# An encoder layer on one core: the first projection in pieces of two token tiles, and another order of three engines before the first recurrent gates

## The chip, the cores and the metric

The kernel runs on 1 core of a Trainium2 chip. The metric is the device time of one execution in microseconds (us), here the median of several. The engines work in parallel, each through its own instruction queue in order, and wait for one another on semaphores: TensorE (PE, its weight loads are PEld), VectorE (DVE), ScalarE (ACT), GpSimd (POOL), and SyncE (SP), which issues the transfers.

## The reference, cut to what matters

One layer over 2304 tokens (2048 of one sequence, 256 of another) with 1024 features, and a final norm:

```python
h = rmsnorm(x, norm1_g)
z = h @ w_in                       # 14 column tiles of 128
u_pool, u_lru, u_gate, u_conv = z[..., :o1], z[..., o1:o2], z[..., o2:o3], z[..., o3:]
y_pool = pool_mixer(u_pool, pool_w, pool_scale)
c = depthwise_conv(u_lru, lru_conv_w, lru_conv_b, 2, 1)          # 4 taps
y_lru = (rg_lru(c, ..., False) + rg_lru(c, ..., True)) * gelu(u_gate)
a, g = split(u_conv)                                             # conformer_conv
v = depthwise_conv(a * sigmoid(g), dw_w, dw_b, 15, 15)           # 31 taps
v = silu(group_norm(v, gn_g, gn_b, 4))
y_conv = v @ pw_w + pw_b                                         # 256 -> 256
x = x + concat([y_pool, y_lru, y_conv]) @ w_out
x = x + expert_choice_ffn(rmsnorm(x, norm2_g), ...)              # 16 experts
return rmsnorm(x, final_g)
```

## The kernel before

Channels lie on the 128 partitions and the tokens along the free dimension. `rows[:, r, :]` is one row tile: 128 channels by all 2304 tokens, with padding (2320 elements between `LO` and `HI`). TensorE's work on a row is cut in the five segments of `SEG`: four of 512 tokens and one of 256. Segment `s` uses PSUM bank `s`; ScalarE moves it to `rows` (an evacuation). `seg_full` counts filled segments, `seg_out` evacuated ones, and a matmul group into a bank waits for the evacuation of what was there.

The order of work is written out by hand, engine by engine. The stages that the change touches:

1. **Norm and first projection.** 18 token tiles of 128 are loaded. For each, ScalarE squares it in four parts (`n1_squares`, L763), TensorE sums these with one small matmul (`n1_stat_of`, L1053), ScalarE takes the root (`n1_root`, L768), and VectorE takes the reciprocal, scales the tile and transposes it into `normT` (L1351, L1363; `n1_tr` counts). Meanwhile TensorE projects two column tiles, g = 0 (`a0`) and g = 1 (the gate `g0`), from `w_ring[:, g]` (`first_piece`, L1066). Each segment and g has 8 matmuls in two halves of four, and one statistic matmul is issued behind every half. Segment `s` waits for tiles up to 4s + 3. ScalarE evacuates (`first_evac`, L774). The last sequence part of g has the sigmoid applied straight from PSUM, the rest in one pass over the row (L789). Behind them ScalarE takes Abs and Exp of the `lambda` vectors (L799, L800), from which VectorE works out a softplus on 128 x 8 (L1381 to L1395).
2. **31-tap convolution.** VectorE multiplies `a` by the sigmoid (L1414), then runs 31 taps over the full row (L1417, L1420), for channel tile 0 and then for tile 1. Between taps 9 and 10, and 20 and 21, of tile 1 it subtracts the group means of tile 0 (`centre`, L1407). Meanwhile TensorE projects the tiles `G_A1`, `G_G1`, `G_P0`, `G_P1`, `G_U`, `G_GT` (`z_tile`, L1098) and works out group means (`mean_of`, L1115) and variances (`var_of`, L1122).
3. **From the last tap to the first gates.** For channel tile i: `gn_mult` (VectorE, L1456), `gn_affine` (ScalarE, two row passes, L831 and L833), `gn_silu` (VectorE, L1461; `gn_out` counts). Between them lie the pool mixer (`pool_mix`, VectorE, L1470 to L1486; `G_PM0`, `G_PM1` on TensorE), the pointwise projection (`G_PW0`, `G_PW1`, `pw_sb`: each of the two outputs sums over both channel tiles), and the preparation of the first recurrent tile: `lru_conv` (four taps over `G_U`'s row, L1437, L1439), and the high and low parts of `u` and of the gate weights (`u_high`, L846; `bd_high`, L841; and L1447, L1450 on VectorE). ScalarE waits for the stores of rows 2 and 4 (`mix_st[2]`, `mix_st[3]`) before the loop.
4. **Loop over four recurrent tiles** (`lru_tile`): four gates (TensorE L1085, ScalarE L899) and two further column tiles (TensorE L1098). The output projection, the router, the experts (16, the largest part) and the final norm follow.

`evac` in the tables of the profile is L806, `gn_square` L817, `gn_scale`'s last pass L824.

Of the kernel before, what the change touches and what calls it, by code (L numbers as in the profile page):

```python
# [22 lines left out]
F32 = mybir.dt.float32  # L23
# [60 lines left out]
N_X, N_SQ, N_LEAD = 6, 3, 6  # L84
# [51 lines left out]
def encoder_layer(nc, x, consts, vecs, norm1_g, w_in, pool_w, lru_wa, lru_wx, conv_pw_w, w_out,  # L136
                  norm2_g, router_w, w_gate, w_up, w_down, final_g, y):
    ctx = ExitStack()
    with ctx:
# [188 lines left out]
        n1_xld = [sem_of(f"n1_xld{q}") for q in range(N_X)]  # L328
        n1_squared, n1_stat = sem_of("n1_squared"), sem_of("n1_stat")
# [56 lines left out]
        first_bank = lambda g, s: 2 * g + s % 2  # L386

# [42 lines left out]
        def _(sp_eng):  # L430
# [75 lines left out]
            store_row(4, 7, 3)  # L506
# [170 lines left out]
        def _(pool):  # L677
# [12 lines left out]
            e.wait_ge(seg_full, NS * (G_PW1 + 1))  # L690
# [59 lines left out]
        def _(act):  # L750
# [20 lines left out]
            def first_evac(g, s, func=ACT.Identity):  # L771
                t0, c0, n = SEG[s]
                e.wait_ge(seg_full, 2 * s + g + 1)
                e.activation(rows[:, g, c0:c0 + n], ps[:, first_bank(g, s), 0:n], func).then_inc(seg_out, 1)  # L774
# [6 lines left out]
            for t in range(2, NT):  # L781
# [3 lines left out]
                if t >= 7 and t % 2 == 1:  # L785
                    first_evac((t - 7) // 2 % 2, (t - 7) // 4)
            done = SEG[NS - 2][1]
            e.wait_ge(seg_out, 2 * NS - 4)
            e.activation(rows[:, 1, PAD:done], rows[:, 1, PAD:done], ACT.Sigmoid).then_inc(glu_sig, 1)  # L789
            for s in range(NS - 2, NS):  # L790
                first_evac(0, s)
                first_evac(1, s, ACT.Sigmoid)

# [6 lines left out]
            e.activation(sp[:, 1, :, :], sp[:, 0, :, :], ACT.Exp, scale=-1.0).then_inc(sp_ready, 1)  # L800

# [55 lines left out]
            evac(G_GT, 8, ACT.Identity, between=((0, lambda: gn_affine(0)), (3, lambda: gn_square(1))))  # L857
            gn_scale(1)
            evac(G_PM0, 10, ACT.Identity, scale=vec[:, V_PSC:V_PSC + 1])
            gn_affine(1)  # L860
            evac(G_PM1, 11, ACT.Identity, scale=vec[:, V_PSC + 1:V_PSC + 2])
# [26 lines left out]
            def lru_tile(l, last):  # L888
# [151 lines left out]
        def _(pe):  # L1040
# [15 lines left out]
            def first_piece(s, g, half):  # L1056

                t0, c0, n = SEG[s]
                if half == 0 and s >= 2:
                    e.wait_ge(seg_out, 2 * (s - 2) + g + 1)  # L1060
                if half == 0 and g == 0:
                    e.wait_ge(n1_tr, min(4 * s + 4, NT))
                if half == 0 and s == 0:
# [855 lines left out]
```

## Time and profile before

| what | value |
|---|---|
| median of 3 runs | 2691.8 us (2690.86 to 2691.93) |
| the profiled execution's own time | 2687.19 us |
| its span, first to last instruction | 2685.3 us |
| busy: PE / DVE / ACT / POOL | 2484.8 / 1749.7 / 1137.1 / 493.3 us |
| mean granted TensorE clock | 0.966 of full speed |

The profiled execution is 4.6 us shorter than the median of the runs. Instants in the rows further down are from the start of its span. The stages above take the first 357.5 us up to the first `z_tile` of the loop; all that follows is the same program in both kernels but for one wait and one call that is split in two.

### The profile page before, as it was taken

Reading aid. Unit: us, or ns where it says so; the run is one execution under the profiler, and the core shown is the slowest. Engines: PE = TensorE matmul, PEld = TensorE weight load, DVE = VectorE, ACT = ScalarE, POOL = GpSimd, SP = SyncE. Lnnn points to the kernel's source line nnn.
Section 4 is the critical chain, followed back from the end, with each engine's and each line's share of the span. In section 5 each row is a group of like instructions: output and inputs, shape, how many; then the busy total and the mean of one; then the engine's idle time right before and its main releaser. Section 6 shows DMA issues by size and latency. Waiting matters only on the chain.

```text
span 2685.3 us, 42869 instructions
## 1 busy us (share of the span) xinstructions
PE 2484.8 (93%) x15834; PEld 2185.8 (81%) x15834; DVE 1749.7 (65%) x2114; ACT 1137.1 (42%) x1645; POOL 493.3 (18%) x347
## 2 busy tenths in 40 slices
PE   6999899989996299999999999999999999999990
PEld 3544455558786299999999999999999999999980
DVE  6699766678456676666656765756666667557544
ACT  5102555552232144454444444444544444444433
POOL 0000033310000112132132131321321321312201
PEclk9999999999997599999999999999999999999995
DMA  8000111137765176686776866866867767768638
GB/s 174 24 16 9 53 36 35 35 127 219 263 229 169 57 200 165 191 210 158 205 196 158 219 175 166 226 166 190 216 161 196 205 160 208 188 162 223 168 82 296
DMA packets 656264, 425.30 MB, mean 158 GB/s; under 512 B 30592, under 2 KB 633216, under 8 KB 655104
## 3 DMA queue, kind: packets, MB, share of 16 engines
q1 hardware_dynamic: 628480, 385.46, 49.7%
q0 software_dynamic: 27648, 37.77, 7.4%
q8 instruction: 117, 1.92, 0.3%
q14 instruction: 19, 0.16, 0.0%
HBM read 357.09 MB, written 66.06 MB: 158 GB/s over the span
## 4 chain that ended last, share of the span: by engine, by line
PE 83%; DVE 11%; issue 2%; ACT 2%; DMA 2%; SPq 1%; POOL 0%; ACTq 0%; DVEq 0%; POOLq 0%
PE ps L1302 42%; PE ps L1319 21%; PE ps L1098 7%; DVE rows L1420 6%; PE ps L1174 4%; PE ps L1189 4%; PE ps L1066 2%; PE ps L1206 1%; DMA fin_x<-resid 1%; PE ps L1085 1%; DVE over_t L1676 1%; ACT rows L899 1%; PE ps L1047 1%; DVE wo_l L1505 0%; SPq L450 0%
## 5 line engine op out<-in xcount | busy, mean ns | idle before, releaser
L1302 PE MATMUL ps<-x_h,w_l 128*128 128x288 f32 x2816 | 831.2, 295 | 18.6 <-issue 18.6
L1302 PE MATMUL ps<-x_l,w_h 128*128 128x288 f32 x2816 | 829.9, 295 | 0.0
L1302 PE MATMUL ps<-x_h,w_h 128*128 128x288 f32 x2816 | 829.7, 295 | 0.0
L1707 DVE TENSOR_TENSOR w_l<-raw,w_h 128x1024 fp32r<-128x1024 f32 (+1 forms) x480 | 637.4, 1328 | 277.3 <-ACT w_h L982 276.7
L982 ACT ACTIVATE w_h<-raw 128x1024 fp32r<-128x1024 f32 (+1 forms) x480 | 545.4, 1143 | 453.1 <-PE ps L1319 272.4
L1302 PEld LDWEIGHTS ps<-x_h,w_l 128*128 128x128 f32 x2816 | 530.0, 188 | 18.7 <-issue 18.7
L1302 PEld LDWEIGHTS ps<-x_l,w_h 128*128 128x128 f32 x2816 | 530.2, 188 | 0.0
L1302 PEld LDWEIGHTS ps<-x_h,w_h 128*128 128x128 f32 x2816 | 530.1, 188 | 0.0
L734 POOL DMA_INDIRECT resid<-y_rows,idx_cur x144 | 250.2, 1738 | 964.9 <-ACT y_rows L997 930.4
L1319 PE MATMUL ps<-h_l,w_h 128*128 128x288 f32 x1408 | 414.4, 294 | 0.0
L1319 PE MATMUL ps<-h_h,w_h 128*128 128x288 f32 x1408 | 414.4, 294 | 0.0
L1319 PE MATMUL ps<-h_h,w_l 128*128 128x288 f32 x1408 | 414.4, 294 | 0.0
L1098 PE MATMUL ps<-normT,w_ring 128*128 128x512 f32 (+1 forms) x960 | 372.9, 550 | 2.1 <-issue 1.1
L1098 PEld LDWEIGHTS ps<-normT,w_ring 128*128 128x128 f32 x960 | 182.5, 190 | 190.7 <-issue 184.4
L1319 PEld LDWEIGHTS ps<-h_h,w_h 128*128 128x128 f32 x1408 | 264.6, 188 | 0.0
L1319 PEld LDWEIGHTS ps<-h_h,w_l 128*128 128x128 f32 x1408 | 264.6, 188 | 0.0
L1319 PEld LDWEIGHTS ps<-h_l,w_h 128*128 128x128 f32 x1408 | 264.5, 188 | 0.0
L719 POOL DMA_INDIRECT gathered<-tokens,idx_next x144 | 153.7, 1067 | 580.6 <-issue 379.3
L1009 ACT ACTIVATE sig<-ps 128x288 f32<-128x288 f32 x176 | 72.1, 410 | 291.1 <-PE ps L1302 291.0
L1789 DVE TENSOR_TENSOR h_l<-hid,h_h 128x288 fp32r<-128x288 f32 x176 | 80.5, 457 | 149.2 <-ACT h_h L1014 147.6
L1814 DVE STREAM_TRANSPOSE y_rows<-ps 128x288 f32<-128x288 f32 x128 | 61.7, 482 | 161.3 <-PE ps L1319 160.2
L1420 DVE SCALAR_TENSOR_TENSOR rows<-rows,vec 128x2320 f32<-128x2320 f32 x60 | 158.1, 2635 | 2.1
(230 smaller groups left out, 2484.7 us busy)
## 6 DMA issues: line engine op xcount, KB each, us to landing
raw<-w_gate SPq DMA_DIRECT2D x176, 512.0 KB, 4.2
raw<-w_up SPq DMA_DIRECT2D x176, 512.0 KB, 4.7
raw<-w_down SPq DMA_DIRECT2D x128, 704.0 KB, 5.9
n_x<-x SPq DMA_DIRECT2D x72, 128.0 KB, 5.0
e_x<-x SPq DMA_DIRECT2D x18, 512.0 KB, 4.6
resid<-e_x SPq DMA_DIRECT2D x18, 512.0 KB, 3.0
s_x<-resid SPq DMA_DIRECT2D x18, 512.0 KB, 4.5
resid<-s_r SPq DMA_DIRECT2D x18, 512.0 KB, 3.0
```

Of the source, the lines that this page charges most:

```text
L719: e.indirect_dma_start(gathered[:, c, :], None, token_parts, bass.IndirectOffsetOnAxis(ap=idx_next[:, c:c + 1], axis=0)).then_inc(x_got[c ...
L734: e.indirect_dma_start(resid_parts, bass.IndirectOffsetOnAxis(ap=idx_cur[:, c:c + 1], axis=0), y_rows[:, c, :], None, compute_op=ALU.add). ...
L982: e.activation(w_h[:, m % SPLIT, 0:k * P], raw[:, m % RAW, 0:k * P], ACT.Copy).then_inc(hi_done, 1)
L1009: e.activation(sig[:, j % 2, :], ps[:, 2 * (j % 2), 0:SLOTS], ACT.Sigmoid).then_inc(sig_done, 1)
L1098: ins = e.matmul(ps[:, s, 0:n], w_ring[:, slot, k, :], normT[:, k, t0:t0 + n], start=k == 0, stop=k == KD - 1)
L1174: ins = e.matmul(ps[:, early_bank(t, h), :], lhs[t % E_MIX][:, m, :], rhs[:, k, cols], start=n == 1, stop=n == 12)
L1189: ins = e.matmul(ps[:, 1 + 2 * p + h, :], lhs[:, p, k, :], rhs[:, 2 + k, cols], start=n == 1, stop=n == 3 * LK)
L1302: ins = e.matmul(ps[:, bank, 0:SLOTS], lhs(k), rhs[:, k, 0:SLOTS], start=m == 1, stop=m == 3 * KD)
L1319: ins = e.matmul(ps[:, bank, 0:SLOTS], lhs(k), rhs[:, k, 0:SLOTS], start=m == 1, stop=m == 3 * KF)
L1420: ins = e.scalar_tensor_tensor(out=rows[:, c, mid], in0=rows[:, v, LO - 15 + k:HI - 15 + k], scalar=tap(k), in1=rows[:, c, mid], op0=ALU.m ...
L1707: e.tensor_tensor(w_l[:, m % SPLIT, 0:k * P], raw[:, m % RAW, 0:k * P], w_h[:, m % SPLIT, 0:k * P].bitcast(F32), ALU.subtract).then_inc(lo ...
L1789: e.tensor_tensor(h_l[:, j, 0:SLOTS], hid[:, j % 2, :], h_h[:, j, 0:SLOTS].bitcast(F32), ALU.subtract).then_inc(hl_done, 1)
```

## The change

The first projection is cut in 18 pieces of 256 tokens (`PAIR`), g = 0 and g = 1 by turns, each of 8 matmuls of 128x256, each waiting for two token tiles; it has semaphores of its own (`first_full`, `first_out`). ScalarE takes Abs and Exp, and the sigmoid pass over `g0`, before its last four evacuations. Between the last tap and the gates VectorE, ScalarE and TensorE run in another order, the pointwise projection is split in the part of channel tile 0 and that of tile 1, its second output goes to row 5 instead of 4, and the wait for the stores moves into the loop, ahead of the first write to these rows.

```diff
-N_X, N_SQ, N_LEAD = 6, 3, 6
+N_X, N_SQ, PAIR = 6, 3, 2 * P
+N_SEG = T // PAIR
...
+        first_cols = lambda s: (PAIR * s, PAD + PAIR * s if PAIR * s < SAMPLE else SEQ[1][0])
+        pw_bank = lambda j, s: (NS * j + s) % 8
...
             def w_load(n, c):
-                if n == 2:
-                    e.wait_ge(seg_full, 2 * NS - 1)
-                elif n > 2:
+                if n in (2, 3):
+                    e.wait_ge(first_full, 2 * N_SEG - 3 + n)
+                elif n > 3:
...
-            store_row(4, 7, 3)
+            store_row(5, 7, 3)
...
             e.wait_ge(gn_out, 2)
-            e.wait_ge(seg_full, NS * (G_PW1 + 1))
             e.memset(rows[:, 0:6, PAD + SAMPLE:PAD + SAMPLE + PAD], 0.0).then_inc(rows_zeroed, 1)
...
             def first_evac(g, s, func=ACT.Identity):
-                t0, c0, n = SEG[s]
-                e.wait_ge(seg_full, 2 * s + g + 1)
-                e.activation(rows[:, g, c0:c0 + n], ps[:, first_bank(g, s), 0:n], func).then_inc(seg_out, 1)
+                t0, c0 = first_cols(s)
+                e.wait_ge(first_full, 2 * s + g + 1)
+                e.activation(rows[:, g, c0:c0 + PAIR], ps[:, first_bank(g, s), 0:PAIR], func).then_inc(first_out, 1)
...
-                if t >= 7 and t % 2 == 1:
-                    first_evac((t - 7) // 2 % 2, (t - 7) // 4)
-            done = SEG[NS - 2][1]
-            e.wait_ge(seg_out, 2 * NS - 4)
-            e.activation(rows[:, 1, PAD:done], rows[:, 1, PAD:done], ACT.Sigmoid).then_inc(glu_sig, 1)
-            for s in range(NS - 2, NS):
-                first_evac(0, s)
-                first_evac(1, s, ACT.Sigmoid)
-
+                if t >= N_X + 1:
+                    first_evac((t - N_X - 1) % 2, (t - N_X - 1) // 2)
+            for n in range(NT - N_X - 1, 2 * N_SEG - 4):
+                first_evac(n % 2, n // 2)
             e.wait_ge(cst_ld, 16)
             e.wait_ge(vec_ld, 16)
...
             step.link(e.activation(sp[:, 0, :, :], lam, ACT.Abs))
             e.activation(sp[:, 1, :, :], sp[:, 0, :, :], ACT.Exp, scale=-1.0).then_inc(sp_ready, 1)
+            done = first_cols(N_SEG - 2)[1]
+            e.wait_ge(first_out, 2 * N_SEG - 4)
+            e.activation(rows[:, 1, PAD:done], rows[:, 1, PAD:done], ACT.Sigmoid).then_inc(glu_sig, 1)
+            for s in range(N_SEG - 2, N_SEG):
+                first_evac(0, s)
+                first_evac(1, s, ACT.Sigmoid)
+            e.sem_inc(seg_out, 2 * NS)
...
-            evac(G_GT, 8, ACT.Identity, between=((0, lambda: gn_affine(0)), (3, lambda: gn_square(1))))
+            evac(G_GT, 8, ACT.Identity, between=((0, lambda: (gn_affine(0), gn_square(1))),))
             gn_scale(1)
             evac(G_PM0, 10, ACT.Identity, scale=vec[:, V_PSC:V_PSC + 1])
+            evac(G_PM1, 11, ACT.Identity, scale=vec[:, V_PSC + 1:V_PSC + 2])
             gn_affine(1)
-            evac(G_PM1, 11, ACT.Identity, scale=vec[:, V_PSC + 1:V_PSC + 2])
             bd_high(0)
             for s in (0, 1):
                 e.wait_ge(mix_st[s], 32)
-            for i in range(2):
-                e.wait_ge(gn_out, i + 1)
-                evac(G_PW0 + i, C[i], ACT.Identity, bias=vec[:, V_PWB + i:V_PWB + i + 1],
-                     between=((1, lambda: u_high(0)),) if i == 1 else ())
-            for s in (2, 3):
-                e.wait_ge(mix_st[s], 32)
+            u_high(0)
+            e.wait_ge(gn_out, 2)
+            for j in range(2):
+                for s, (t0, c0, n) in enumerate(SEG):
+                    e.wait_ge(seg_full, NS * (G_PW0 + j) + s + 1)
+                    e.activation(rows[:, (2, 5)[j], c0:c0 + n], ps[:, pw_bank(j, s), 0:n], ACT.Identity,
+                                 bias=vec[:, V_PWB + j:V_PWB + j + 1]).then_inc(seg_out, 1)
...
                     r, ex = rows[:, 3 * d, LO:HI], rows[:, 3 * d + 2, LO:HI]
+                    e.wait_ge(mix_st[2 + d], 32)
                     step.link(e.activation(ex, r, ACT.Exp, scale=spc(6, d)))
...
-            for n in range(4 * NS):
-                first_piece(n // 4, n // 2 % 2, n % 2)
-                if N_LEAD + n < NT:
-                    n1_stat_of(N_LEAD + n)
+            for n in range(2 * N_SEG):
+                first_piece(n // 2, n % 2)
+                if N_X + n < NT:
+                    n1_stat_of(N_X + n)
+            e.sem_inc(seg_full, 2 * NS)
...
-            z_first(G_GT, 7, between=((0, lambda: mean_of(1, 0, 1, 2)), (1, lambda: mean_of(1, 3, 4))))
+            z_first(G_GT, 7, between=((0, lambda: mean_of(1, 0, 1, 2, 3, 4)),))
...
+            places = [(j, s) for j in range(2) for s in range(NS)]
+            e.wait_ge(gn_out, 1)
+            for n, (j, s) in enumerate(places[:8]):
+                if n < NS:
+                    e.wait_ge(seg_out, NS * G_PM1 + s + 1)
+                pw_mat(0, j, s)
             e.wait_ge(gn_out, 2)
-            for j in range(2):
-                segments(G_PW0 + j, lambda s, t0, c0, n: [
-                    (pw_sb[:, i, j * P:(j + 1) * P], rows[:, (0, 3)[i], c0:c0 + n]) for i in range(2)])
+            for j, s in places[:8]:
+                pw_mat(1, j, s).then_inc(seg_full, 1)
+            for n, (j, s) in enumerate(places[8:]):
+                e.wait_ge(seg_out, NS * G_PW0 + n + 1)
+                pw_mat(0, j, s)
+                pw_mat(1, j, s).then_inc(seg_full, 1)
+            e.wait_ge(seg_out, NS * (G_PW1 + 1))
...
+            centre(1, 0, 1, 2)
             gn_mult(0)
-            centre(1, 0, 1, 2, 3, 4)
+            centre(1, 3, 4)
+            pool_mix(0)
             gn_silu(0)
-            pool_mix(0)
             pool_mix(1)
             gn_mult(1)
-            gn_silu(1)
             e.wait_ge(seg_out, NS * (G_U + 1))
             lru_conv(0)
+            gn_silu(1)
+            u_low(0)
```

`first_piece(s, g)` is now eight matmuls of 256 tokens that wait for `n1_tr` >= 2s + 2 and, from s = 2 on, for `first_out` >= 2(s - 2) + g + 1. `pw_mat(i, j, s)` is one matmul of input tile i, output j, segment s. `u_low` is the last operation of the old `lru_conv`, now called apart.

Three places of the programs, as the engines have them in their queues. ScalarE at the end of the first projection, before:

```order
L768 ACTIVATE n_dev<-ps 128x4 x2
L774 ACTIVATE rows<-ps 128x512
L789 ACT_TABLE_LOAD
L789 ACTIVATE rows<-rows 128x1536
L774 ACTIVATE rows<-ps 128x512 x2
L774 ACTIVATE rows<-ps 128x256 x2
L799 ACTIVATE sp<-vec 128x8
L800 ACT_TABLE_LOAD
L800 ACTIVATE sp<-sp 128x8
L806 ACTIVATE rows<-ps 128x512 x4
```

and now (`sp` is the softplus scratch, L777 the evacuation of a piece, L811 that of `G_A1`):

```order
L771 ACTIVATE n_dev<-ps 128x4
L777 ACTIVATE rows<-ps 128x256 x4
L797 ACTIVATE sp<-vec 128x8
L798 ACT_TABLE_LOAD
L798 ACTIVATE sp<-sp 128x8
L801 ACT_TABLE_LOAD
L801 ACTIVATE rows<-rows 128x1792
L777 ACTIVATE rows<-ps 128x256 x4
L811 ACTIVATE rows<-ps 128x512 x4
```

Abs and Exp have moved ahead of the last four evacuations, and the row pass of the sigmoid stands behind them.

VectorE from the last operation of the pool mixer to the loop, before (`gn_mult(1)` L1456, `gn_silu(1)` L1461, the four taps, then the two low parts):

```order
L1486 SCALAR_TENSOR_TENSOR rows<-rows,cst 128x2320
L1456 TENSOR_TENSOR rows<-rows 128x2320
L1461 TENSOR_TENSOR rows<-rows 128x2320
L1437 TENSOR_SCALAR rows<-rows,vec 128x2320
L1439 SCALAR_TENSOR_TENSOR rows<-rows,vec 128x2320 x3
L1447 TENSOR_TENSOR bd_parts<-bd_w,bd_parts 128x512
L1450 TENSOR_TENSOR u_parts<-rows,u_parts 128x2320
```

and now (`gn_mult(1)` L1482, taps L1461 and L1463, `gn_silu(1)` L1487, `u_low` L1476):

```order
L1512 SCALAR_TENSOR_TENSOR rows<-rows,cst 128x2320
L1482 TENSOR_TENSOR rows<-rows 128x2320
L1461 TENSOR_SCALAR rows<-rows,vec 128x2320
L1463 SCALAR_TENSOR_TENSOR rows<-rows,vec 128x2320 x3
L1471 TENSOR_TENSOR bd_parts<-bd_w,bd_parts 128x512
L1487 TENSOR_TENSOR rows<-rows 128x2320
L1476 TENSOR_TENSOR u_parts<-rows,u_parts 128x2320
```

The second silu product has moved behind the four taps and the low part of the weights.

TensorE from the pool projections to the loop, before:

```order
L1085 MATMUL ps<-rows,bd_pool 128x512 x4
L1085 MATMUL ps<-rows,bd_pool 128x256
L1085 MATMUL ps<-rows,pw_sb 128x512 x8
L1085 MATMUL ps<-rows,pw_sb 128x256 x2
L1085 MATMUL ps<-rows,pw_sb 128x512 x8
L1085 MATMUL ps<-rows,pw_sb 128x256 x2
```

and now (the first two rows of `pw_sb` and seven of the next are the parts of tile 0 and the start of those of tile 1, which wait for `gn_out` 2):

```order
L1092 MATMUL ps<-rows,bd_pool 128x512 x4
L1092 MATMUL ps<-rows,bd_pool 128x256
L1147 MATMUL ps<-rows,pw_sb 128x512 x4
L1147 MATMUL ps<-rows,pw_sb 128x256
L1147 MATMUL ps<-rows,pw_sb 128x512 x7
L1147 MATMUL ps<-rows,pw_sb 128x256
L1147 MATMUL ps<-rows,pw_sb 128x512 x5
L1147 MATMUL ps<-rows,pw_sb 128x256 x2
```

The number of pointwise matmuls is the same, 16 of 512 and 4 of 256; eight of them (7 of 512, 1 of 256) now stand ahead of the wait for the second silu product.

## Rows read from the trace of the kernel before

**Rows 1.** The page: the chain that ended last, shares by engine.

```profile
PE 83%; DVE 11%; issue 2%; ACT 2%; DMA 2%; SPq 1%; POOL 0%; ACTq 0%; DVEq 0%; POOLq 0%
```

**Rows 2.** Instructions in order, 22 to 34 us: start, duration, engine, [idle before].

```profile
25.47 5.53 PE L1066 MATMUL ps<-normT,w_ring 128*128 128x512 f32 x8 [1.16 <-DVE normT L1351]
...
29.91 0.19 ACT L763 ACTIVATION_READ_ACCUMULATOR n_sq<-n_x 128x1 f32 x1
...
30.84 0.28 PE L1053 MATMUL ps<-n_ss,same_tok 128*128 128x4 f32 x2
```

**Rows 3.** Instructions in order, 60 to 110 us, ScalarE and VectorE.

```profile
85.22 0.60 ACT L774 ACTIVATE rows<-ps 128x512 f32<-128x512 f32 x1 [6.27 <-PE ps L1066]
...
92.12 0.38 ACT L774 ACTIVATE rows<-ps 128x256 f32<-128x256 f32 x1 [3.07 <-PE ps L1066]
...
97.38 2.57 DVE L1414 TENSOR_TENSOR rows<-rows 128x2320 f32<-128x2320 f32 x1
```

**Rows 4.** Instructions in order, 200 to 280 us, TensorE.

```profile
210.63 1.53 PE L1115 MATMUL ps<-rows,cst 128*128 128x512 f32 x4 [1.25 <-DVE rows L1407]
...
257.10 7.03 PE L1098 MATMUL ps<-normT,w_ring 128*128 128x512 f32 x16
268.63 4.27 PE L1115 MATMUL ps<-rows,cst 128*128 128x512 f32 x6 [4.50 <-DVE rows L1420]
```

**Rows 5.** Instructions in order, 280 to 330 us, VectorE.

```profile
280.66 1.02 DVE L1407 TENSOR_TENSOR rows<-rows,ps 128x512 f32<-128x512 f32 x2 [7.04 <-PE ps L1115]
...
284.08 2.60 DVE L1470 TENSOR_TENSOR rows<-rows 128x2351 f32<-128x2351 f32 x1
...
293.85 2.61 DVE L1470 TENSOR_TENSOR rows<-rows 128x2351 f32<-128x2351 f32 x1
...
308.89 2.58 DVE L1456 TENSOR_TENSOR rows<-rows 128x2320 f32<-128x2320 f32 x1
316.21 2.57 DVE L1461 TENSOR_TENSOR rows<-rows 128x2320 f32<-128x2320 f32 x1 [4.74 <-ACT rows L833]
318.70 1.48 DVE L1437 TENSOR_SCALAR rows<-rows,vec 128x2320 f32<-128x2320 f32 x1
...
328.12 0.69 DVE L1447 TENSOR_TENSOR bd_parts<-bd_w,bd_parts 128x512 fp32r<-128x512 f32 x1
```

**Rows 6.** Instructions in order, 300 to 430 us, ScalarE.

```profile
305.94 2.77 ACT L806 ACTIVATE rows<-ps,vec 128x512 f32<-128x512 f32 x5
...
311.51 2.32 ACT L831 ACTIVATE rows<-rows,vec 128x2320 f32<-128x2320 f32 x1 [1.50 <-DVE rows L1456]
...
341.73 1.28 ACT L891 ACT_TABLE_LOAD   x1 [4.96 <-DMA mixed<-rows]
...
344.74 3.36 ACT L899 ACTIVATE rows<-ps,vec_l 128x512 f32<-128x512 f32 x6
...
423.10 8.14 ACT L899 ACTIVATE rows<-ps,vec_l 128x512 f32<-128x512 f32 x15
```

**Rows 7.** Instructions in order, 290 to 435 us, TensorE.

```profile
298.08 4.03 PE L1122 MATMUL ps<-rows,cst 128*128 128x512 f32 x10
...
318.84 17.43 PE L1085 MATMUL ps<-rows,pw_sb 128*128 128x512 f32 x40 [4.09 <-ACT rows L806]
...
345.48 11.76 PE L1085 MATMUL ps<-u_parts,bd_parts 128*128 128x512 f32 x45 [4.49 <-ACT rows L899]
357.50 62.11 PE L1098 MATMUL ps<-normT,w_ring 128*128 128x512 f32 x160 [0.26 <-ACT rows L899]
...
433.90 62.11 PE L1098 MATMUL ps<-normT,w_ring 128*128 128x512 f32 x160 [0.38 <-ACT rows L899]
```

**Rows 8.** Stretches of 1 us: length, PE busy (instructions), granted clock, DMA.

```profile
320.00:321.00 1.00, 1.00 (x2) 0.50 1.10 451
...
348.00:349.00 1.00, 1.00 (x3) 0.50 0.00 0
```

**Rows 9.** The page's costliest groups: weight loads of the column tiles.

```profile
L1098 PEld LDWEIGHTS ps<-normT,w_ring 128*128 128x128 f32 x960 | 182.5, 190 | 190.7 <-issue 184.4
```

More of the change, by code:

```diff
@@ L328, in encoder_layer @@
         n1_xld = [sem_of(f"n1_xld{q}") for q in range(N_X)]
+        first_full, first_out = sem_of("first_full"), sem_of("first_out")
         n1_squared, n1_stat = sem_of("n1_squared"), sem_of("n1_stat")
@@ L1054, in n1_stat_of, with first_piece @@
                          start=True, stop=True).then_inc(n1_stat, 1)
[L1056 to L1063, printed above, removed]
+            def first_piece(s, g):
+                t0, c0 = first_cols(s)
+                if g == 0:
+                    e.wait_ge(n1_tr, 2 * s + 2)
+                if s >= 2:
+                    e.wait_ge(first_out, 2 * (s - 2) + g + 1)
+                if s == 0:
                     e.wait_ge(w_ld[g], 16 * PARTS)
-                for k in range(4 * half, 4 * half + 4):
-                    ins = e.matmul(ps[:, first_bank(g, s), 0:n], w_ring[:, g, k, :], normT[:, k, t0:t0 + n],
+                for k in range(KD):
+                    ins = e.matmul(ps[:, first_bank(g, s), 0:PAIR], w_ring[:, g, k, :], normT[:, k, t0:t0 + PAIR],
                                    start=k == 0, stop=k == KD - 1)
-                if half == 1:
-                    ins.then_inc(seg_full, 1)
+                ins.then_inc(first_full, 1)
             e.wait_ge(same_set, 1)
-            for t in range(N_LEAD):
+            for t in range(N_X):
                 n1_stat_of(t)
-            for n in range(4 * NS):
-                first_piece(n // 4, n // 2 % 2, n % 2)
-                if N_LEAD + n < NT:
-                    n1_stat_of(N_LEAD + n)
+            for n in range(2 * N_SEG):
[3 more added lines that the diff above has]
+            e.sem_inc(seg_full, 2 * NS)
             def segments(g, mats):
@@ L1093, in z_tile @@
                     if isinstance(g, int) and g == G_A1:
-                        e.wait_ge(seg_out, 2 * NS - (s == 0))
+                        e.wait_ge(first_out, 2 * N_SEG - (s < 2))
                     else:
@@ L1137, in _, with pw_mat @@
                 segments(G_PM0 + i, lambda s, t0, c0, n: [(bd_pool[:, i, :], rows[:, 10 + i, c0:c0 + n])])
-            e.wait_ge(gn_out, 2)
-            for j in range(2):
-                segments(G_PW0 + j, lambda s, t0, c0, n: [
-                    (pw_sb[:, i, j * P:(j + 1) * P], rows[:, (0, 3)[i], c0:c0 + n]) for i in range(2)])
+            def pw_mat(i, j, s):
+                t0, c0, n = SEG[s]
+                return e.matmul(ps[:, pw_bank(j, s), 0:n], pw_sb[:, i, j * P:(j + 1) * P],
+                                rows[:, (0, 3)[i], c0:c0 + n], start=i == 0, stop=i == 1)
+            places = [(j, s) for j in range(2) for s in range(NS)]
[4 more added lines that the diff above has]
+                pw_mat(0, j, s)
+            e.wait_ge(gn_out, 2)
+            for j, s in places[:8]:
[5 more added lines that the diff above has]
+            e.wait_ge(seg_out, NS * (G_PW1 + 1))
             def lru_tile(l, last):
@@ L1409, in _ @@
             for i in range(2):
-                e.wait_ge(seg_out, NS * (2 * i + 2))
                 if i == 0:
                     e.wait_ge(glu_sig, 1)
+                    e.wait_ge(first_out, 2 * N_SEG)
+                else:
+                    e.wait_ge(seg_out, NS * (G_G1 + 1))
                 v, c = V[i], C[i]
@@ L1448, in lru_conv, with u_low @@
                                 ).then_inc(bd_lo, 1)
+            def u_low(l):
                 e.wait_ge(u_hi, l + 1)
-                e.tensor_tensor(u_parts[:, 1, mid], c, u_parts[:, 0, mid].bitcast(F32), ALU.subtract
+                e.tensor_tensor(u_parts[:, 1, mid], rows[:, 9, mid], u_parts[:, 0, mid].bitcast(F32), ALU.subtract
                                 ).then_inc(u_lo, 1)
@@ L1587, in lru_tile @@
                     lru_conv(l + 1)
+                    u_low(l + 1)
                     e.wait_ge(mix_st[4], 32 * (l + 1))
```

## The prediction, made before the changed kernel was run

> **What bounds the kernel.** I read the chain of work first: it lies 83% on TensorE and 11% on VectorE [rows 1], and VectorE's part is the 31-tap convolution. Then the instructions in order, engine by engine, to see who waits for whom at the joints of the first 357.5 us. There the bound changes hands: TensorE up to the end of the first projection; VectorE from the start of the convolution at 97.38 [rows 3] to its last tap at 268.6, where TensorE has waited 4.50 us [rows 4]; then a mixed chain of VectorE, ScalarE and TensorE to the first `z_tile` of the loop at 357.50 [rows 7]. From there TensorE runs through, and the two programs are the same. So I ask only how much earlier that `z_tile` starts. No transfer or engine behind it has a clock of its own, so the rest shifts with it.
>
> **Start of the first projection.** Before, the first piece starts at 25.47, after 1.16 us of waiting for the fourth tile [rows 2]. Now it needs two tiles, but stands behind the statistic of tile 5 on TensorE's queue, so it can start at 24.3. The piece is as long as before (eight half-wide matmuls for four wide ones), 5.4 us from its start to the next statistic matmul, 25.47 to 30.84: 29.7. That statistic, of tile 6, needs squares that end at 30.10 (29.91 + 0.19) [rows 2]; these wait for the tile's transfer, which is not moved. So it starts at about 30.15: 0.7 us earlier than before, not 1.2. Later tiles are never late: piece n needs tile n + 1, whose statistic stands behind piece n - 5.
>
> Wide: 8 matmuls of 512 tokens take 6.87 us (6.27 + 0.60, ScalarE's interval between evacuations); 8 of 256 take 3.45 (3.07 + 0.38) [rows 3]. A piece costs 3.45 where half a segment cost 3.435, so 16 pieces add 0.3 us. The stage ends 0.4 us earlier.
>
> On this the Trainium skill speaks against the change. "TensorE: Matmul & The Clock Gate", section "Back-to-back issue gap", adds a fixed 2.5 ns to every pass at full clock. Twice as many matmuls are 64 more; if each makes four passes that is an estimate of 0.6 us, where the rows make it 0.3. The forecast would be 0.3 us longer.
>
> **Start of the convolution.** Before, ScalarE's last evacuation ends at 92.50 and VectorE starts the product only at 97.38 [rows 3]: 4.9 us for Abs, a table load, Exp and the softplus chain. Now Abs and Exp come after the evacuation of piece 13, when four pieces (13.8 us) are still to run. ScalarE's two table loads and the row pass take about 5 us of this and delay one evacuation, which nothing waits for: a piece waits for the evacuation four pieces back. VectorE is idle then. It starts at 92.50 - 0.4 + 0.05 = 92.15, which is 5.2 earlier. If that cover were gone, the 4.9 would be back.
>
> The convolution's own work is the same, so the last tap ends at 268.6 - 5.2 = 263.4. Does TensorE arrive in time? It starts `G_A1` 0.4 earlier (its weights still wait for the last g = 0 piece), and the wait of 1.25 us for `centre` at 210.63 [rows 4] goes, since VectorE is now 5.2 ahead there. Its first `G_GT` segment ended at 264.13 (257.10 + 7.03) [rows 4]; now at 262.5. It waits 0.9 us instead of 4.5, and I expect no fall of its clock there. A shift beyond 6.1 would gain nothing more without TensorE.
>
> **From the last tap to the gates.** I count from the last tap, L (268.6 before, 263.4 now).
> - Means: 4.27 us for three wide matmuls after the idle time, at the low clock [rows 4]; 2.58 at full clock (0.86 each, 6.87 / 8). All five means now come together, 3.9 us, then three segments of 6.87 and one of 3.45: the variances start at L + 28.0 (L + 29.5 before: 298.08 [rows 7]).
> - From there ScalarE needs 7.9 us to the end of `gn_scale(1)` (305.94 - 298.08 [rows 6, 7]): L + 35.9.
> - VectorE: three `centre` to L + 3.4, `gn_mult(0)` 2.5, two `centre` 1.0 [rows 5] to L + 6.9; `pool_mix(0)` 9.8 (293.85 - 284.08); `gn_silu(0)` 2.5, whose factors ScalarE has at about L + 10.6; `pool_mix(1)` 15.0 (308.89 - 293.85), to L + 34.2. It waits for `gn_scale(1)`, and `gn_mult(1)` ends at L + 38.5. Then the taps, 9.4 us (328.12 - 318.70), to L + 47.9, the weights' low part 0.6, and `gn_silu(1)` 2.5 [rows 5] ends at L + 51.1. Behind it waits only `u_low`, done at L + 53.6, before anybody asks for it.
> - ScalarE: `G_PM0` 2.8 [rows 6] to L + 38.7, `G_PM1` at TensorE's pace to L + 41.2, a table load 1.3, `gn_affine(1)` two passes of 2.3 [rows 6] to L + 47.1, `bd_high`, then `u_high` from L + 48.0 (the taps' end) to L + 50.2. `gn_silu(1)` has its factors 1.4 us before VectorE is there, and the place of the old wait for them (4.74 us at 316.21 [rows 5]) is filled with the taps. The stores of rows 10 and 11 end before u_conv does.
> - TensorE: `G_PM1` to L + 40.4, the eight first halves of the pointwise projection 6.45 us (7.5 wide matmuls) to L + 46.9. It waits 4.2 us for `gn_out` 2 at L + 51.1. Before, this was L + 50.2 (318.84), 0.9 earlier. Then eight second halves, 6.45, and the last two places, 2.6 (3 wide matmuls). Before, the 20 matmuls took 17.43 where full clock gives 15.5: a loss of 1.9 after 4.09 us idle [rows 7], with the granted clock at 0.50, the 1.2 GHz level, at 320 [rows 8]. With 4.2 us idle I take the same 1.9. Fill ends at L + 62.1, ScalarE's last evacuation at L + 62.7; before, L + 68.2. Gain 5.5.
> - The stores: before, ScalarE stood 4.96 us for them at 341.73 [rows 6]. Now their wait is ahead of the first write to rows 2 and 5, some 13 us into the gates; issue and landing take 5. SP's next step, the weights of the loop, comes earlier with all else and lands some 5 us before its use. Gain 4.9.
> - ScalarE from there to its first gate evacuation: 3.0 (344.74 - 341.73) [rows 6], as before: L + 65.7. GpSimd's cube, which ScalarE needs in the middle of the gates, follows the last pointwise evacuation by 9.2 us and has 1.7 to spare.
> - Gates: before, 12.76 us to the `z_tile` (344.74 to 357.50), since TensorE had waited 4.49 us and ran its 45 matmuls in 11.76 [rows 6, 7], at 0.50 [rows 8]. In the second round, without that, 10.80 (423.10 to 433.90) [rows 6, 7]. Now TensorE is only 3 us ahead of ScalarE and waits 0.4: 10.8. Gain 2.0.
>
> The `z_tile` starts at L + 76.5 = 339.9, 17.6 us earlier: 5.2 ahead of the tap and 12.4 behind it (88.9 - 76.5). The profiled execution, 2687.2, becomes 2669.6. The median of the runs is 4.6 longer, so 2674.2; I say 2674.
>
> A place where page and trace differ: "ScalarE: Activation LUTs", section "What ACT_TABLE_LOAD costs", of the Trainium skill says a load drains the engine as well, 2.66 us in all; the trace has 1.28 with the next instruction right behind. By the page `gn_affine(1)` would end 1.4 later and `bd_high` would hold up VectorE: an estimate of 2675.
>
> **Bounds.** The clock after the 4.2 us: no fall gives 1.9 less, a fall that lasts half again as long 1.0 more. The start: 0.2 to 1.2 for my 0.7. Small waits in the new chain that I have at nothing (GpSimd's 1.7, semaphores between engines): up to 3.
>
> **Rivals.**
> - *TensorE's clock falls once more*, ahead of the gates or before the last tap, as before (each 1.9). For it: idle times are still there (0.9, 4.2, 0.4). Against: the two short ones are like the 1.25 at 210.63, where the four records took 1.53, full speed [rows 4]. 2676.1. Chance 0.12.
> - *TensorE's clock doesn't fall at all.* 2672.3. Chance 0.10; 4.09 us idle was enough at 318.84.
> - *The new order gives nothing behind the tap*: `gn_silu(1)` stands behind the taps, and ScalarE's pointwise evacuations behind `u_high`. Were one of them 12 us later than reckoned, only the head's 5.2 is left: 2686.6. Against: the slack of `u_high` is 2.7 us (first full place L + 52.9), and every operand but one has a row. Chance 0.07, with parts of this loss (2680 and up) included.
> - *Slower: weight loads no longer hidden.* The pieces of 256 need 64 more matmuls with two loads each of 0.190 us [rows 9]: 24.3 us if none hides, so 2691.8 - 17.6 + 24.3 = 2698.5. It decides from 73% of them in the open. Against: eight half-wide matmuls, loads included, already take 3.45 us, half of 6.87 and 0.015 [rows 3]. Chance 0.02.
> - *No effect*, because a wait later in the loop takes all back: no such wait is seen in the chain. Chance 0.03.
>
> **Numbers.** The forecast has the remaining 0.66. The range goes from 2669 (no fall, start 1.2 early, other terms 2 better) to 2680 (the second fall, 3 of small waits, a little of the third rival). A measurement can tell about 0.2%, 5.4 us, from no change: faster means below 2686.4. Faster 0.93, same 0.05, slower 0.02.
>
> **What would show it.** The convolution's product starts at about 92.15 right behind the last evacuation; the last tap at 263.4, with TensorE's wait under 1.5 us and the three means in 2.7; `gn_silu(1)` without a wait, ending at 314.5; TensorE's wait of 4 us before the second halves; no wait of ScalarE for `mixed` before the gates; first gate evacuation at 329, `z_tile` at 340; then the same distances as before. It would be wrong if `G_A1` started late, if ScalarE were not done with Abs, Exp and the row pass before the last piece, or if a new wait showed between `gn_out` 2 and the gates.

## The result and the profile after

| what | before | after |
|---|---|---|
| median | 2691.33 us (4 runs, 2687.83 to 2691.93) | 2672.22 us (4 runs, 2671.19 to 2673.70) |
| the profiled execution's own time | 2687.19 us | 2673.06 us |
| its span | 2685.3 us | 2671.2 us |
| first `z_tile` of the loop starts | 357.50 us | 340.44 us |

The ratio is 0.9933, 95% interval 0.9921 to 0.9945, so 14.8 to 21.3 us less: below 1%, but clear of the spread of the runs. The forecast was 2674 (2669 to 2680), from 17.6 us less at the first `z_tile`.

The kernel after, VectorE's instructions in order: the softplus chain's first operation, the product that begins the convolution, and the joint behind the last tap (start, duration, and in brackets the idle time before and who ended it).

```profile
80.35 0.17 DVE L1403 TENSOR_SCALAR sp<-sp 128x8 f32<-128x8 f32 x1 [4.21 <-ACT sp L798]
...
92.61 2.58 DVE L1438 TENSOR_TENSOR rows<-rows 128x2320 f32<-128x2320 f32 x1 [8.95 <-ACT rows L777]
...
299.93 2.58 DVE L1482 TENSOR_TENSOR rows<-rows 128x2320 f32<-128x2320 f32 x1 [1.89 <-ACT rows L829]
...
303.94 7.98 DVE L1463 SCALAR_TENSOR_TENSOR rows<-rows,vec 128x2320 f32<-128x2320 f32 x3
311.87 0.69 DVE L1471 TENSOR_TENSOR bd_parts<-bd_w,bd_parts 128x512 fp32r<-128x512 f32 x1
312.48 2.57 DVE L1487 TENSOR_TENSOR rows<-rows 128x2320 f32<-128x2320 f32 x1
```

The product starts at 92.61 where it was 97.38 [rows 3]; its releaser is the last evacuation, no longer the softplus. At L1487, `gn_silu(1)`, there is no wait; before, 4.74 us stood there [rows 5].

TensorE of the same kernel. Compare with [rows 2, 4, 7].

```profile
24.19 6.06 PE L1073 MATMUL ps<-normT,w_ring 128*128 128x256 f32 x16
30.44 0.39 PE L1060 MATMUL ps<-n_ss,same_tok 128*128 128x4 f32 x2 [0.18 <-ACT n_sq L766]
...
255.61 7.03 PE L1105 MATMUL ps<-normT,w_ring 128*128 128x512 f32 x16
263.87 4.13 PE L1122 MATMUL ps<-rows,cst 128*128 128x512 f32 x10 [1.22 <-DVE rows L1444]
...
291.89 4.03 PE L1129 MATMUL ps<-rows,cst 128*128 128x512 f32 x10
...
304.50 6.60 PE L1147 MATMUL ps<-rows,pw_sb 128*128 128x512 f32 x16
315.10 10.98 PE L1147 MATMUL ps<-rows,pw_sb 128*128 128x512 f32 x24 [4.00 <-DVE rows L1487]
327.09 12.97 PE L1092 MATMUL ps<-u_parts,bd_parts 128*128 128x512 f32 x60 [1.00 <-ACT rows L875]
340.44 62.11 PE L1105 MATMUL ps<-normT,w_ring 128*128 128x512 f32 x160 [0.38 <-ACT rows L905]
```

The last tap ends at 263.82 (268.6 before). The wait ahead of the means is 1.22 us instead of 4.50, and all five means take 4.13, as long as three took before. Of the pointwise projection only 24 records stand behind `gn_silu(1)`; 40 did. All 60 records of the gates run in one piece of 12.97 us: the hole of 4.49 us is gone. The `z_tile` starts 17.06 us earlier.

ScalarE of the same kernel: the table load ahead of `gn_affine(1)`, and further down the joint to the loop, with no wait for a transfer ahead of the loop's first table load, where it stood 4.96 us [rows 6]:

```profile
305.34 1.28 ACT L836 ACT_TABLE_LOAD   x1
306.64 2.32 ACT L836 ACTIVATE rows<-rows,vec 128x2320 f32<-128x2320 f32 x1
...
326.12 0.47 ACT L875 ACTIVATE rows<-ps,vec 128x256 f32<-128x256 f32 x1 [0.18 <-PE ps L1147]
326.62 1.28 ACT L897 ACT_TABLE_LOAD   x1
...
329.63 8.15 ACT L905 ACTIVATE rows<-ps,vec_l 128x512 f32<-128x512 f32 x15
```

**The spans differ by 14.1 us, not 17.1.** The rest of the program is the same, but its length isn't constant. From the `z_tile` to the 312 records that stand in the chain of waits for the first expert it took 606.1 us in the profiled execution of before and 609.0 in that of after:

```profile
357.50 62.12 PE ps L1098 x160
...
963.57 41.19 PE ps L1302 x312
```

(before), and after:

```profile
340.44 62.12 PE ps L1105 x160
...
949.48 41.19 PE ps L1324 x312
```

In the ten profiled executions of this study it lies between 606.1 and 609.6, and before's is the lowest. The two differ between the first output matmuls and the last router logits; from the 312 records on the distances are alike again. Near the end of that stretch one group of 16 logit records takes 1.96 us in before and 2.48 in after, and the transposes behind it 1.10 against 1.95. Before:

```profile
842.25 1.96 PE L1206 MATMUL ps<-router,s_hT 128*128 128x16 f32 x16 [1.81 <-ACT s_hT L956]
844.06 1.10 PE L1047 MATMUL ps<-cst,s_h 128*128 128x128 f32 x8
```

and after:

```profile
826.45 2.48 PE L1228 MATMUL ps<-router,s_hT 128*128 128x16 f32 x16 [1.81 <-ACT s_hT L963]
828.77 1.95 PE L1054 MATMUL ps<-cst,s_h 128*128 128x128 f32 x8
```

The granted clock fell to 0.50 within the second of these rows in before, and already within the first in after. The two rows hold 1.4 of the 3.0 us. Another 0.8 lies between the first large set of output matmuls and the second, where TensorE stands 1.46 us in before and 2.35 in after; why, the profile doesn't show. So one pair of executions may be off by some 3 us in what the change doesn't touch, and only the medians or the position of the `z_tile` say what it is worth.

### The profile page after: what moved, and what is told of

It is laid out like the page before. It is cut to its first block, busy times and chain, and to the rows that moved or that the text cites. A ratio compares the mean times of both kernels' runs of the same rounds, so it can differ in the third digit from the quotient of the medians.

```text
span 2671.2 us, 43140 instructions
## 1 busy us (share of the span) xinstructions
PE 2481.7 (93%) x15962; PEld 2208.9 (83%) x15962; DVE 1750.3 (66%) x2114; ACT 1136.5 (43%) x1652; POOL 490.9 (18%) x347
## 4 chain that ended last, share of the span: by engine, by line
PE 83%; DVE 10%; issue 2%; ACT 2%; DMA 2%; SPq 1%; POOL 0%; ACTq 0%; DVEq 0%; POOLq 0%
PE ps L1324 42%; PE ps L1341 21%; PE ps L1105 8%; DVE rows L1444 6%; PE ps L1196 4%; PE ps L1211 4%; PE ps L1073 2%; PE ps L1228 1%; DMA fin_x<-resid 1%; ACT rows L905 1%; DVE over_t L1705 1%; PE ps L1054 1%; SPq L454 0%; PE ps L1147 0%; DVE wo_l L1533 0%
```

## The experiments

The theory is the prediction's: four gains add up at the `z_tile`, namely the softplus chain off the path ahead of the convolution, eight pointwise matmuls ahead of their wait, the stores' wait hidden, and with it the low clock of the gates. The rivals are that the pieces of 256 tokens, the order of silu and taps, or the clock carry more or less than that. Times of the `z_tile` are from each kernel's trace. Medians beside it are of 4 to 10 runs a kernel; the medians of before in the two sets were 2690.45 (8 runs, experiments 1 to 4) and 2689.72 (15 runs, 5 to 8), against 2691.33 beside the changed kernel. So a difference from the changed kernel's 2672.22 holds up to 1.6 us that aren't the edit's. The ratios of experiments 1 to 4 are 0.9953 to 0.9958, with intervals that begin at 0.9937 to 0.9943 and so just overlap the changed kernel's, which ends at 0.9945. What each edit is worth is therefore read from the `z_tile`, and the median only agrees with it.

**1. The softplus behind the last evacuation again** (one edit undone in the changed kernel).

```diff
+            done = first_cols(N_SEG - 2)[1]
+            e.wait_ge(first_out, 2 * N_SEG - 4)
+            e.activation(rows[:, 1, PAD:done], rows[:, 1, PAD:done], ACT.Sigmoid).then_inc(glu_sig, 1)
+            for s in range(N_SEG - 2, N_SEG):
+                first_evac(0, s)
+                first_evac(1, s, ACT.Sigmoid)
...
             step.link(e.activation(sp[:, 0, :, :], lam, ACT.Abs))
             e.activation(sp[:, 1, :, :], sp[:, 0, :, :], ACT.Exp, scale=-1.0).then_inc(sp_ready, 1)
-            done = first_cols(N_SEG - 2)[1]
-            e.wait_ge(first_out, 2 * N_SEG - 4)
-            e.activation(rows[:, 1, PAD:done], rows[:, 1, PAD:done], ACT.Sigmoid).then_inc(glu_sig, 1)
-            for s in range(N_SEG - 2, N_SEG):
-                first_evac(0, s)
-                first_evac(1, s, ACT.Sigmoid)
```

> Abs and Exp go back behind ScalarE's last evacuation of the first projection; all else as in the changed kernel. Theory (the gain ahead of the tap is the softplus chain alone, and the convolution's start carries through to the first z_tile): VectorE's product starts at 97.4 instead of 92.6, the last tap moves by 4.8 us and so does the first z_tile of the loop, 340.4 to about 345.2; TensorE then waits some 6 us for the last tap and its clock falls there, which may cost up to 1.5 us more. Median about 2677 to 2678.5. Rival (the pieces of 256 carry part of the head's gain): the product starts before 97.0.

Median 2678.44, 6.2 above the changed kernel. VectorE's product in this kernel:

```profile
97.48 2.57 DVE L1438 TENSOR_TENSOR rows<-rows 128x2320 f32<-128x2320 f32 x1
```

and TensorE's means, second halves and `z_tile`:

```profile
268.72 6.50 PE L1122 MATMUL ps<-rows,cst 128*128 128x512 f32 x10 [4.50 <-DVE rows L1444]
...
322.33 12.16 PE L1147 MATMUL ps<-rows,pw_sb 128*128 128x512 f32 x24 [4.00 <-DVE rows L1487]
...
348.83 62.11 PE L1105 MATMUL ps<-normT,w_ring 128*128 128x512 f32 x160 [0.37 <-ACT rows L905]
```

The product is at 97.48, 4.87 later: the softplus chain is the whole gain ahead of the tap, and the pieces, still in this kernel, save nothing without it. The `z_tile` is 8.39 later. Of this 4.86 is the tap, 2.4 the means (6.50 for 4.13), which now follow 4.50 us of idle time, and 1.2 the second halves (12.16 for 10.98). So 3.5 us go to the clock, where I had allowed up to 1.5; the `z_tile` at 348.83 lies beyond what I expected, though the median is still in its range.

**2. The stores' wait ahead of the loop again.**

```diff
+            for s in (2, 3):
+                e.wait_ge(mix_st[s], 32)
             e.wait_ge(rows_zeroed, 7)
...
-                    e.wait_ge(mix_st[2 + d], 32)
```

> The wait for the stores of the pointwise rows goes back ahead of the loop; all else as in the changed kernel. Theory: ScalarE stands about 4.9 us for the transfer, TensorE is idle for about 4.5 of them and runs the gates partly at the low clock, 2 us more: the first z_tile at 347.3, median about 2679. Rival (the wait costs only its own length): z_tile at 345.3, median 2677.

Median 2678.93, 6.7 above the changed kernel. TensorE:

```profile
327.56 3.41 PE L1093 MATMUL ps<-u_parts,bd_parts 128*128 128x512 f32 x15 [0.98 <-ACT rows L875]
335.87 11.77 PE L1093 MATMUL ps<-u_parts,bd_parts 128*128 128x512 f32 x45 [4.90 <-ACT rows L907]
347.90 62.11 PE L1106 MATMUL ps<-normT,w_ring 128*128 128x512 f32 x160 [0.26 <-ACT rows L907]
```

The hole, 4.90 us, and the slow 45 records, 11.77 us, are back. The `z_tile` is 7.46 later, 0.5 of it from the start of the kernel (the product at 93.12). The theory's 6.9 holds; the rival, the wait's own length of 4.9 alone, falls.

**3. All pointwise matmuls behind `gn_out` 2 again.**

```diff
-            e.wait_ge(gn_out, 1)
+            e.wait_ge(gn_out, 2)
             for n, (j, s) in enumerate(places[:8]):
...
                 pw_mat(0, j, s)
-            e.wait_ge(gn_out, 2)
-            for j, s in places[:8]:
                 pw_mat(1, j, s).then_inc(seg_full, 1)
```

> All 20 pointwise matmuls wait for the second silu product again; all else as in the changed kernel. Theory: eight first halves, 6.45 us, come behind the wait: z_tile at 346.9, median about 2678.7. TensorE is idle for over 10 us and its clock falls as it does with 4.0. Rival (the longer idle time costs a longer stretch at the low clock): 1 to 2 us more.

Median 2678.01, 5.8 above. On TensorE the 40 records take 18.14 us after an idle time of 10.43:

```profile
315.11 18.14 PE L1147 MATMUL ps<-rows,pw_sb 128*128 128x512 f32 x40 [10.43 <-DVE rows L1485]
...
347.58 62.11 PE L1105 MATMUL ps<-normT,w_ring 128*128 128x512 f32 x160 [0.35 <-ACT rows L905]
```

The `z_tile` is 7.14 later: 6.45 for the matmuls and 0.7 for the clock, which loses 2.6 here (18.14 - 15.5) and 1.9 in the changed kernel (10.98 - 9.05). The rival's 1 to 2 us more aren't there, and the 0.7 can't be put down to the longer idle time: in experiments 1 and 6 the loss is 3.1 and 3.3 after only 4.0 us.

**4. The silu product ahead of the four taps again.**

```diff
+            gn_silu(1)
             e.wait_ge(seg_out, NS * (G_U + 1))
             lru_conv(0)
-            gn_silu(1)
             u_low(0)
```

> VectorE takes the second silu product ahead of the four taps again, with the evacuations of the pointwise projection still behind u_high. Theory: VectorE idles until ScalarE's affine ends at L + 47.1, the taps end at L + 59.1 and u_high at L + 61.3; ScalarE evacuates the eight full banks only then, and the last place is out at about L + 67: 4.3 us later, z_tile at 344.7, median about 2676.5. Rival (the order of silu and taps doesn't matter, since the pointwise projection fills sooner): no change, 340.4.

Median 2677.56, 5.3 above. TensorE has its second halves 1.4 us earlier, fills eight banks and then waits for ScalarE, which is held by `u_high` (TensorE in order):

```profile
313.67 9.72 PE L1147 MATMUL ps<-rows,pw_sb 128*128 128x512 f32 x16 [2.87 <-DVE rows L1487]
325.97 4.54 PE L1147 MATMUL ps<-rows,pw_sb 128*128 128x512 f32 x8 [2.58 <-ACT rows L875]
...
344.85 62.11 PE L1105 MATMUL ps<-normT,w_ring 128*128 128x512 f32 x160 [0.36 <-ACT rows L905]
```

The `z_tile` is 4.41 later, as reckoned. ScalarE sets the pace here, ten evacuations behind `u_high` with only 0.22 us of waiting between them: the 16 records took 9.72 us after 2.87 of idle time, where the first halves take 6.60 at full clock, and this cost nothing, since they filled the banks before ScalarE came. So silu ahead of the taps pays nothing while the evacuations stand behind `u_high`; a kernel with both orders turned wasn't run.

**5. TensorE kept at work ahead of the second silu product** (a new edit on the changed kernel; four matmuls are added, whose results are overwritten).

```diff
             e.wait_ge(gn_out, 1)
+            for j, s in places[:4]:
+                e.wait_ge(seg_out, NS * G_PM1 + s + 1)
+                t0, c0, n = SEG[s]
+                e.matmul(ps[:, pw_bank(j, s), 0:n], pw_sb[:, 0, j * P:(j + 1) * P], rows[:, 0, c0:c0 + n],
+                         start=True, stop=True)
             for n, (j, s) in enumerate(places[:8]):
```

> The changed kernel with four matmuls more (128x512, their results are overwritten) ahead of the first halves of the pointwise projection, so that TensorE's idle time before the second silu product falls from 4.0 us to about 0.6. Theory (the clock falls because of this idle time, and costs 1.9 us): the 24 records behind the wait take 9.1 us instead of 10.98, z_tile at 338.5, median about 2670.3. Rival (the clock falls anyway, or ScalarE's evacuations set the pace): z_tile at 340.4, or up to 0.5 later because the extra matmuls push the first halves past the product.

Median 2670.41 (2668.44 to 2673.40, 5 runs), 1.8 below the changed kernel; the ratios' intervals overlap (0.9915 to 0.9942), so the runs alone don't show it. The trace does:

```profile
304.46 3.60 PE L1155 MATMUL ps<-rows,pw_sb 128*128 128x512 f32 x8
307.89 6.60 PE L1147 MATMUL ps<-rows,pw_sb 128*128 128x512 f32 x16
315.05 9.29 PE L1147 MATMUL ps<-rows,pw_sb 128*128 128x512 f32 x24 [0.56 <-DVE rows L1492]
...
338.67 62.11 PE L1105 MATMUL ps<-normT,w_ring 128*128 128x512 f32 x160 [0.35 <-ACT rows L905]
```

The idle time is 0.56 instead of 4.00, the 24 records take 9.29 instead of 10.98, and the `z_tile` is 1.77 earlier. The idle time is what costs the 1.9 us: nearly all of it is gone with it, 1.7 of 1.9 in the 24 records.

**6. Four statistic matmuls instead of six ahead of the first piece.**

```diff
-N_X, N_SQ, PAIR = 6, 3, 2 * P
+N_X, N_SQ, N_LEAD, PAIR = 6, 3, 4, 2 * P
...
-            for t in range(N_X):
+            for t in range(N_LEAD):
                 n1_stat_of(t)
...
-                if N_X + n < NT:
-                    n1_stat_of(N_X + n)
+                if N_LEAD + n < NT:
+                    n1_stat_of(N_LEAD + n)
```

(and `N_LEAD` for `N_X` in ScalarE's order of roots and evacuations.)

> The changed kernel with four instead of six statistic matmuls ahead of the first piece. Theory (the first piece is held by its place in TensorE's queue, behind the statistic of tile 5, whose tile lands late): it starts at 18 to 19.5 instead of 24.2, the convolution's product at 87 and z_tile at about 334.8; median about 2666.5. Rival (transfers bind: pieces then wait for token tiles or weights): the start is earlier but the last piece ends where it did, less than 1 us gained.

Median 2666.80 (5 runs, 2664.87 to 2669.17), 5.4 below the changed kernel. TensorE in this kernel:

```profile
17.76 5.94 PE L1073 MATMUL ps<-normT,w_ring 128*128 128x256 f32 x16 [0.81 <-DVE normT L1373]
...
24.82 3.72 PE L1073 MATMUL ps<-normT,w_ring 128*128 128x256 f32 x16 [1.01 <-DMA w_ring<-w_in]
...
299.11 6.60 PE L1147 MATMUL ps<-rows,pw_sb 128*128 128x512 f32 x16
309.71 12.32 PE L1147 MATMUL ps<-rows,pw_sb 128*128 128x512 f32 x24 [3.99 <-DVE rows L1487]
...
336.36 62.11 PE L1105 MATMUL ps<-normT,w_ring 128*128 128x512 f32 x160 [0.38 <-ACT rows L905]
```

and VectorE's product:

```profile
87.22 2.57 DVE L1438 TENSOR_TENSOR rows<-rows 128x2320 f32<-128x2320 f32 x1 [6.38 <-ACT rows L777]
```

The first piece starts 6.4 us earlier, its successor then waits 1.01 for weights, and the product is 5.4 earlier, as expected. The `z_tile` is only 4.1 earlier (336.36, not 334.8), since the second halves take 12.32 after an idle time of 3.99: the clock cost 3.3 us where it cost 1.9 in the changed kernel.

**7. The kernel before with the pieces alone.** The hunks on `PAIR`, `w_load`, `first_evac` and `first_piece` of the diff, with the sigmoid pass and the last evacuations still ahead of Abs and Exp, and the old order behind the tap.

> The kernel before with the pieces of two token tiles alone (Abs and Exp behind the last evacuation, the old order from the last tap on). Theory: the first piece starts 1.3 us earlier, but waits for tile 6's squares and costs 0.02 to 0.03 us more each: the last piece ends at 92.1, z_tile at 357.5, no change. Rival (pieces give what the other parts don't): product before 96.5.

Median 2690.44 (10 runs) against 2689.72 (15 runs): ratio 1.0002, 0.9993 to 1.0011. No effect, as forecast. The product starts at 97.29:

```profile
97.29 2.57 DVE L1421 TENSOR_TENSOR rows<-rows 128x2320 f32<-128x2320 f32 x1
```

and TensorE's means and pointwise matmuls:

```profile
268.54 5.30 PE L1120 MATMUL ps<-rows,cst 128*128 128x512 f32 x6 [4.50 <-DVE rows L1427]
...
319.79 18.16 PE L1090 MATMUL ps<-rows,pw_sb 128*128 128x512 f32 x40 [4.10 <-ACT rows L811]
```

Its `z_tile` is at 359.36, 1.9 later than before's, though the tap is 0.1 earlier: 1.0 in the means (5.30 for 4.27) and 0.7 in the pointwise matmuls (18.16 for 17.43), after the same idle times. The edit doesn't touch these; it is how long the low clock lasted: ahead of the pointwise matmuls it was at 0.50 from about 318.0 to 324.7, and in before from 319.3 to 322.7. So the expected `z_tile` at 357.5 was missed by the clock, not by the pieces. The softplus chain moved without the pieces wasn't run; that the pieces aren't needed for its gain is likely from this and experiment 1, but not shown.

**8. Experiments 5 and 6 together.**

> The two edits of e5 and e6 together. Theory: they lie in different stages and add up: z_tile at about 332.9, median about 2664.6. Rival (a shift of one joint uncovers another bound, so that they add up to less): z_tile after 333.9.

Median 2663.50 (4 runs, 2661.74 to 2664.89), 0.9899 of before (0.9884 to 0.9915): the fastest of the study, 26 us below before and 8.7 below the changed kernel; its interval ends where the changed kernel's (from 0.9921) has not begun. TensorE's second halves and `z_tile`:

```profile
310.27 9.29 PE L1147 MATMUL ps<-rows,pw_sb 128*128 128x512 f32 x24 [0.56 <-DVE rows L1492]
...
333.91 62.11 PE L1105 MATMUL ps<-normT,w_ring 128*128 128x512 f32 x160 [0.39 <-ACT rows L905]
```

The product was at 87.77, 4.8 earlier than in the changed kernel, and the `z_tile` 6.53 earlier: 4.8 and 1.77 add up. It stands 1.0 later than the 332.9 I had expected and so, by 0.01 us, within the rival's condition (after 333.9). But no new bound is seen: 0.8 of the 1.0 is there already at the product (87.77 for 87), and behind it TensorE has no wait that experiments 5 and 6 don't have.

## Why the prediction was right

**Sign, size and mechanism.** 17.6 us were reckoned up to the `z_tile`, 17.06 measured. With L the last tap (263.82), `gn_silu(1)` ended at L + 51.2 (51.1 reckoned), the last pointwise evacuation at L + 62.8 (62.7), the first gate evacuation began at L + 65.8 (65.7), the `z_tile` at L + 76.6 (76.5). The 12.4 behind the tap came out at 12.3. The median is 1.8 us under the forecast, which is within the spread of the runs.

**What was luck.** The step from the `z_tile` to the median didn't hold in detail. The profiled execution took 2673.06 where 2669.6 was reckoned: 0.5 of the difference is the `z_tile`, 3.0 the unchanged rest. And it was not 4.6 us below the median, as in before, but 0.8 above it. The two errors go against each other. Luck too is the 1.9 us for the fall of the clock: experiments 1 and 6 lost 3.1 and 3.3 after the same idle time, more than the 1.0 extra that the bounds allowed.

**Start of the first projection.** Here the term of 0.4 us earlier was mis-sized; it was nothing. Both last pieces end at 92.09. The start at 24.19 and the wait for tile 6's squares were there. But ScalarE began these squares at 28.68, behind its wait for the tile's transfer, where it was 28.39 in before, so the statistic started at 30.44 and not at 30.15, and it took 0.39 us where before's took 0.28. The first piece was longer too, 6.06 us for the 5.4 that I had. The reason isn't shown, the granted clock reads 1.00 in both kernels there, and it wasn't what counted: in experiment 7 the piece took 5.46 and TensorE then stood 0.71 for the squares, with the statistic at 30.35. The pieces cost what was reckoned: 3.676 us each with their statistic (ten of them from 34.22 to 70.98) against 3.657. Over 8 records more a piece that is 2.4 ns a record.
**Start of the convolution.** 5.2 reckoned, 4.77 measured, the difference being the 0.4 above. Experiment 1 gives the softplus chain 4.87 by itself.

**Stores and second clock fall.** 4.9 and 2.0 reckoned, 6.95 together in experiment 2. Hiding the wait is worth more than its length, since TensorE stood behind it.

**Pointwise split.** Reckoned as 5.5 net. Experiments 3 and 4 show that it needs both: the first halves ahead of the wait (7.1) and the new order of silu, taps and `u_high` (4.4). They don't add, since each undoes part of the same stretch.

**Table load.** `gn_affine(1)` began at 306.64, right behind a load of 1.28 us (305.34 to 306.62). The 2.66 us that the Trainium skill gives for a switch ("ScalarE: Activation LUTs", section "What ACT_TABLE_LOAD costs") aren't seen, and the estimate of 2675 that hung on it falls.

**Rivals.** The clock fell once, for 1.9 us, as forecast. The short idle times (1.22, 0.78, 1.00) cost nothing. Weight loads stayed hidden: a piece cost 0.02 us more than half a segment, not the 1.5 us that its eight more loads of 0.190 would add in the open.

**What stays open.** When the clock falls and how long it stays low after one idle time: 1.9 to 3.3 us were lost after 4.0 us. The last section shows how the loss follows from the two; the runs don't say what decides them.

## What to carry to other kernels

Where one engine hands the path to another, list what stands in the receiving engine's queue and in its supplier's queue ahead of the hand-over, and move everything that doesn't need the last result ahead of it: here a softplus on 128 x 8 values cost 4.9 us of a 2690 us kernel. A wait for a transfer belongs at the first overwrite of its source, not at a convenient boundary; if TensorE stands behind it, it costs its length and then a stretch at the low clock (4.9 and 2.0 us here). Judge a gain of this size by the position of the first unchanged instruction in the trace as well as by medians, since the unchanged rest differed by up to 3.5 us between the ten profiled executions.

## What the runs showed of the hardware

The loss after an idle time of TensorE varied for the same instructions: 24 records of the pointwise projection took 10.98, 12.16 and 12.32 us after 4.00, 4.00 and 3.99 us of idle time, and 9.29 after 0.56. In the changed kernel the granted clock was at 0.50, the 1.2 GHz level, from about 315.7 to 319.1, in experiment 6 from 309.0 to about 315.8. Stretches of 1 us (length, busy, clock) of the changed kernel:

```profile
315.00:316.00 1.00, 0.90 (x2) 0.85 0.00 0
...
319.00:320.00 1.00, 1.00 (x4) 0.94 0.00 0
```

and of experiment 6:

```profile
308.00:309.00 1.00, 0.00 (x0) 1.00 0.00 0
309.00:310.00 1.00, 0.29 (x1) 0.50 0.00 0
...
315.00:316.00 1.00, 1.00 (x3) 0.58 0.00 0
```

TensorE's last record before the gap ends at 311.10 in the changed kernel (304.50 + 6.60) and at 305.71 in experiment 6 (299.11 + 6.60). So the clock fell 4.6 us behind it in the one, with the new work already running, and 3.3 us behind it in the other, when the work (from 309.71) hadn't come; and it stayed low for 3.4 and 6.8 us. The loss is half of the time that TensorE works at 0.50: 3.4 us of work at the low clock make an estimate of 1.7, for 1.9 measured, and 6.1 us (309.71 to 315.84) one of 3.1, for 3.3 measured.

Shorter idle times aren't safe either. In experiment 4 the 16 records behind 2.87 us took 9.72, for 6.60 at full clock; the 1.22, 0.78 and 1.00 us of the changed kernel cost nothing. So a predicted loss for one fall should have bounds of 1.9 to 3.3 us, and four matmuls of work that nobody needs, put in the gap, take it out.
